# The mLSTM's two products from operands in two fp32r parts, three passes each, with one buffer a head for queries, keys and values

## The reference, cut to what matters

```
qk = silu(causal_depthwise_conv([q_m, k_m]))         # 4 taps, q and k, 1024 channels each
D[t, s]  = cumulated log gates, -inf for s > t       # per head
w[t, s]  = exp(D[t, s] - m[t]) * (q[t] . k[s]) / 16  # scores, weighted
num[t]   = sum_s w[t, s] * v[s]                      # numerators, 256 wide
den[t]   = sum_s w[t, s]
h[t]     = num[t] / max(|den[t]|, exp(-m[t]))
y_a      = sigmoid(o_pre) * layernorm_per_head(h) * g
```

## Time and profile before

| | us |
|---|---|
| median of 3 runs | 1999.2 |
| lowest and highest | 1997.16 and 2002.15 |
| the profiled execution's own time | 1996.38 |
| its span, first to last instruction | 1994.6 |
| PE busy | 1944.7 (98%) |
| DVE busy | 1050.1 (53%) |
| ACT busy | 633.4 (32%) |
| POOL busy | 280.0 (14%) |

### The profile page before, as it was taken

How to read it: one execution, slowest core, us unless ns; L and a number is a source line. 1 busy time by engine, 2 the same in 40 slices (tenths; PEclk the granted TensorE clock), 3 DMA queues, 4 the chain that set the end, 5 groups by cost and what they waited for, 6 DMA issues and landing times.

```text
span 1994.6 us, 23615 instructions
## 1 busy us (share of the span) xinstructions
PE 1944.7 (98%) x9634; PEld 1583.7 (79%) x9634; DVE 1050.1 (53%) x1458; ACT 633.4 (32%) x1054; POOL 280.0 (14%) x176
## 2 busy tenths in 40 slices
PE   7999999999999999999999999999999999999997
PEld 6778888888888888888888778777777878888885
DVE  6776543345455644343345676656676554344344
ACT  4332322233333432222234422233443333222222
POOL 2212210011111111010013000111111121011013
PEclk9999999999999999999999999999999989999998
DMA  4322233332221332323223222221111313223221
GB/s 166 98 74 85 78 92 105 95 85 77 83 64 48 121 95 95 95 95 105 94 86 100 63 74 75 96 74 55 63 59 48 116 53 106 95 96 99 93 91 66
DMA packets 53235, 172.65 MB, mean 87 GB/s; under 512 B 5995, under 2 KB 9523, under 8 KB 53128
## 3 DMA queue, kind: packets, MB, share of 16 engines
q1 hardware_dynamic: 52256, 169.93, 26.8%
q10 hardware_dynamic: 872, 1.22, 0.2%
HBM read 168.91 MB, written 2.22 MB: 86 GB/s over the span
## 4 chain that ended last, share of the span: by engine, by line
PE 87%; DVE 9%; ACT 2%; issue 1%; POOL 0%; DMA 0%; SPq 0%; DVEq 0%
PE PS L1107 26%; PE PS L1109 25%; PE PS L1108 25%; PE PS L1403 1%; PE PS L1204 1%; PE PS L1381 1%; DVE WL L1756 1%; PE PS L1425 1%; PE PS L1242 1%; PE PS L1172 1%; PE PS L1251 1%; PE PS L1265 1%; PE PS L1219 1%; DVE AR L1784 1%; DVE AR L1895 1%
## 5 line engine op out<-in xcount | busy, mean ns | idle before, releaser
L1107 PE MATMUL PS<-HH,WH 128*128 128x512 f32 x1368 | 541.0, 395 | 11.7 <-DVE WL L1756 8.3
L1109 PE MATMUL PS<-HH,WL 128*128 128x512 f32 x1368 | 534.4, 391 | 0.0
L1108 PE MATMUL PS<-HL,WH 128*128 128x512 f32 x1368 | 534.2, 390 | 0.0
L1472 ACT ACTIVATE WH<-RAW 128x1024 fp32r<-128x1024 f32 (+2 forms) x320 | 326.1, 1020 | 390.1 <-PE PS L1109 389.4
L1756 DVE TENSOR_TENSOR WL<-RAW,WH 128x1024 fp32r<-128x1024 f32 (+2 forms) x256 | 316.4, 1236 | 229.2 <-ACT WH L1472 227.4
L1107 PE MATMUL PS<-AH,WH 128*128 128x512 f32 x1096 | 433.0, 395 | 0.5 <-DVE AL L1747 0.5
L1109 PE MATMUL PS<-AH,WL 128*128 128x512 f32 x1096 | 428.1, 391 | 0.0
L1108 PE MATMUL PS<-AL,WH 128*128 128x512 f32 x1096 | 427.9, 390 | 0.0
L1107 PEld LDWEIGHTS PS<-HH,WH 128*128 128x128 f32 x1368 | 258.1, 189 | 66.9 <-DVE WL L1756 8.3
L1109 PEld LDWEIGHTS PS<-HH,WL 128*128 128x128 f32 x1368 | 257.9, 189 | 54.7
L1108 PEld LDWEIGHTS PS<-HL,WH 128*128 128x128 f32 x1368 | 258.4, 189 | 52.2
(11 more groups left out here) (238 smaller groups left out, 1417.0 us busy)
## 6 DMA issues: line engine op xcount, KB each, us to landing
RAW<-wst SPq DMA_DIRECT2D x288, 512.0 KB, 3.4
RAW<-wst SPq DMA_DIRECT2D x16, 384.0 KB, 3.0
RAW<-wst SPq DMA_DIRECT2D x16, 256.0 KB, 2.6
XT<-xT SPq DMA_DIRECT2D x3, 512.0 KB, 7.2
AR<-mx SPq DMA_DIRECT2D x4, 256.0 KB, 6.7
AR<-scr SPq DMA_DIRECT2D x16, 64.0 KB, 4.4
AR<-scr SPq DMA_DIRECT2D x8, 128.0 KB, 5.0
AR<-w SPq DMA_DIRECT2D x2, 512.0 KB, 4.2
```

Source lines behind the costliest of these rows:

```text
L1107: T.matmul(out, wh, XH[:, k, :], start=k == 0, stop=False)
L1108: T.matmul(out, wh, XL[:, k, :], start=False, stop=False)
L1109: m = T.matmul(out, wl, XH[:, k, :], start=False, stop=k == nk - 1)
L1472: t = A.activation(WH[:, i % NW, 0:n], RAW[:, i % NR, 0:n], ACT.Copy, scale=1.0)
```

## The change

Queries, keys, values and the weights of the numerators are each held as a high part (rounded to fp32r) and a low part (what is left). Each matmul of the scores and the numerators becomes three fp32r passes: high with high, high with low, low with high. The numerators have 258 columns.

- ACT rounds: `after` part 3 for qm and km (line 1569 of the changed kernel), part 1 for vm, out of PSUM (line 1575), and `weights_hi`, four instructions a head (line 1631).
- The rest is subtracted on DVE for odd km units (line 1967), for vm out of PSUM (line 1973, in place of the copy) and for `weights_lo`, four a head (line 2079), and on POOL for qm units and even km units (line 2444).
- Queries, keys and values have one buffer for all heads instead of two by turns. The roundings wait until the head before has been read.
- `weights_hi` stands one quarter after `weights`, `weights_lo` three quarters later; the numerators stay where they were.
- A flush is put ahead of each head's scores, so that part 3 is issued; one `flush_all` becomes two `flush`. Tanh gets two buffers, and waits for the low part of the unit two before.

```diff
@@ -114,7 +114,7 @@
...
-PARTS = {"qm": 2, "km": 2, "vm": 1, "om": 1, "va": 1, "ga": 1, "gb": 1, "pb": 1, "small2": 1, "gk": 1, "gv": 1,
+PARTS = {"qm": 3, "km": 3, "vm": 2, "om": 1, "va": 1, "ga": 1, "gb": 1, "pb": 1, "small2": 1, "gk": 1, "gv": 1,
@@ -128,6 +128,12 @@
 def lo_on_pool(i):
     return i in (6, 8) or i % 2 == 1 and i > 1 and UNITS[i][0] in BUSY_DVE
+
+
+def low_on_pool(i):
+
+    name, j, k0, nk = UNITS[i]
+    return name == "qm" or j % 2 == 0
 def unit_of(name, j=0, k0=0):
@@ -433,7 +439,8 @@
     e.gates_1()
     e.sum_bank("sum", 3)
     e.products(3, range(4))
-    flush_all(e)
+    flush(e)
+    flush(e)
     e.products(3, range(4, 8))
     ahead(e, 4)
     e.gates_log()
@@ -484,7 +491,11 @@
         mlstm_scores(e, h)
         fill.quarters(4)
         e.weights(h)
-        fill.quarters(12 if h else 8)
+        fill.quarters(1)
+        e.weights_hi(h)
+        fill.quarters(3)
+        e.weights_lo(h)
+        fill.quarters(8 if h else 4)
         for t in range(4):
             e.hold((*SB, OB)[t], "numer", h, t)
         e.numerators(h)
@@ -501,6 +512,7 @@
 def mlstm_scores(e, h):
     if h < 4:
+        flush(e, False)
         e.add_diagonal(h)
     if h:
         e.turn_bank("hm", h - 1, 0)
@@ -880,10 +897,17 @@
         tab, oh, vecs = part(0, 24), part(24, 1152), part(1176, 1152)
         SLOT = [part(0, 4608), part(4608, 4608)]
-        (hq0, hq1, hk0, hk1, hv0, hv1, so, xc, yc, th_, Mb, Md, vm1, WT, hm, yf_m, acol, ecol, stat, r0, r1, r2,
-         r3) = parts(4608, 1024, 1024, 1024, 1024, 1028, 1028, 1024, 516, 512, 512, 512, 512, 512, 1280, 1024, 512,
+        (_, _, _, _, _, _, so, xc, yc, th_, Mb, Md, vm1, WT, hm, yf_m, acol, ecol, stat, r0, r1, r2,
+         r3) = parts(4608, 1024, 1024, 1024, 1024, 1032, 1032, 1024, 516, 512, 512, 512, 512, 512, 1280, 1024, 512,
                      16, 16, 64, 512, 512, 512, 512)
-        hq, hk, hv = [hq0, hq1], [hk0, hk1], [hv0, hv1]
+
+        QH, QL, KH, KL = (rounded(4608 + 1024 * n, 1024) for n in range(4))
+        VH, VL = (heads_of(rounded(8704 + 1032 * n, 1032)) for n in range(2))
+        th1 = part(2328, 512)
+        wh2, wl2 = (rounded(2840 + 256 * n, 256) for n in range(2))
+        TH = [th_, th1]
+        WTH = [AH[:, 6, :], AH[:, 7, 0:384], wh2, AH[:, 7, 384:512]]
+        WTL = [AL[:, 6, :], AL[:, 7, 0:384], wl2, AL[:, 7, 384:512]]
         MX = [Mb, r3, r1, r0]
         r0, r1, r2, r3 = (x[0:4, :] for x in (r0, r1, r2, r3))
@@ -1192,21 +1222,21 @@
                 t.then_inc(*pe_done["mlstm"].next("columns_turned"))
             def scores(s, h, blocks):
-                q, k = hq[h % 2], hk[h % 2]
-                for c in (0, 1):
-                    pe.wait_ge(*at("mq", unit_of("qm", 2 * h + c)))
-                    pe.wait_ge(*at("mq", unit_of("km", 2 * h + c)))
                 for t_ in blocks:
                     x, a = SCORES[t_]
                     b, n = s.bank["scores", h, x], 512 - 128 * t_
                     s.free("scores", h, x)
                     for c in (0, 1):
-                        t = T.matmul(PS[:, b, a:a + n], k[:, c * 512 + t_ * 128:c * 512 + t_ * 128 + 128],
-                                     q[:, c * 512 + t_ * 128:c * 512 + 512], start=c == 0, stop=c == 1)
+                        keys, queries = (slice(c * 512 + t_ * 128, c * 512 + e_) for e_ in (t_ * 128 + 128, 512))
+                        pe.wait_ge(*at("m_lo", unit_of("qm", 2 * h + c)))
+                        pe.wait_ge(*at("m_hi", unit_of("km", 2 * h + c)))
+                        T.matmul(PS[:, b, a:a + n], KH[:, keys], QH[:, queries], start=c == 0, stop=False)
+                        T.matmul(PS[:, b, a:a + n], KH[:, keys], QL[:, queries], start=False, stop=False)
+                        pe.wait_ge(*at("m_lo", unit_of("km", 2 * h + c)))
+                        t = T.matmul(PS[:, b, a:a + n], KL[:, keys], QH[:, queries], start=False, stop=c == 1)
                     t.then_inc(*pe_done["mlstm"].next("scored", h, t_))
             def numerators(s, h):
-                v = heads_of(hv[h % 2])
                 pe.wait_ge(*at("ones"))
                 pe.wait_ge(*at("free", "tokens", unit_of("vm", 2 * h)))
                 pe.wait_ge(*at("free", "tokens", unit_of("vm", 2 * h + 1)))
@@ -1214,9 +1244,11 @@
                     b = s.bank["numer", h, t_]
                     s.free("numer", h, t_)
                     for x in range(t_ + 1):
-                        o = wo[x] + (t_ - x) * 128
-                        pe.wait_ge(*at("weights", h, x))
-                        t = T.matmul(PS[:, b, 0:257], WT[:, o:o + 128], v[:, x, :], start=x == 0, stop=x == t_)
+                        o = slice((t_ - x) * 128, (t_ - x) * 128 + 128)
+                        pe.wait_ge(*at("weights_lo", h, x))
+                        T.matmul(PS[:, b, 0:258], WTH[x][:, o], VH[:, x, :], start=x == 0, stop=False)
+                        T.matmul(PS[:, b, 0:258], WTH[x][:, o], VL[:, x, :], start=False, stop=False)
+                        t = T.matmul(PS[:, b, 0:258], WTL[x][:, o], VH[:, x, :], start=False, stop=x == t_)
                     t.then_inc(*pe_done["mlstm"].next("summed", h, t_))
             def gated(s, h, j):
@@ -1526,7 +1558,23 @@
                 name, j, k0, nk = UNITS[i]
                 if name in ("qm", "km") and p == 1:
                     act.wait_ge(*at("conv", i, 3))
-                    A.activation(th_, yc, ACT.Tanh, scale=0.5).then_inc(*act_done["mlstm"].next("tanh", i))
+                    if CONVS.index(i) > 1:
+                        act.wait_ge(*at("m_lo", CONVS[CONVS.index(i) - 2]))
+                    A.activation(th_of(i), yc, ACT.Tanh, scale=0.5).then_inc(*act_done["mlstm"].next("tanh", i))
+                elif name in ("qm", "km") and p == 3:
+                    h, c = j // 2, slice(j % 2 * 512, j % 2 * 512 + 512)
+                    act.wait_ge(*at("m_full", i))
+                    if h:
+                        act.wait_ge(*at("scored", h - 1, 3))
+                    t = A.activation((QH if name == "qm" else KH)[:, c], th_of(i), ACT.Copy, scale=1.0)
+                    t.then_inc(*act_done["mlstm"].next("m_hi", i))
+                elif name == "vm" and p == 1:
+                    if j > 1:
+                        act.wait_ge(*at("summed", j // 2 - 1, 3))
+                    act.wait_ge(*at("turned", i))
+                    t = A.activation(VH[:, :, j % 2 * 128:j % 2 * 128 + 128], heads_of(PS[:, s.bank["tokens", i], :]),
+                                     ACT.Copy, scale=1.0)
+                    t.then_inc(*act_done["mlstm"].next("v_hi", i))
                 elif name == "down":
                     act.wait_ge(*at("free", "sum", i))
                     s.scaled_hi("h3", AH, j, XT[:, j, :], GG[:, j:j + 1])
@@ -1565,7 +1613,7 @@
                 act.wait_ge(*at("free", "columns"))
                 act.wait_ge(*at("diagonal", h))
                 if h:
-                    act.wait_ge(*at("summed", h - 1, 3))
+                    act.wait_ge(*at("weights_lo", h - 1, 3))
                 for t_ in range(4):
                     n, o, bias = 512 - 128 * t_, wo[t_], acol[:, 4 * t_ + h:4 * t_ + h + 1]
                     t = A.activation(WT[:, o:o + 128], Md[:, 128 * t_:128 * t_ + 128], ACT.Exp, scale=-1.0, bias=bias)
...
                     t.then_inc(*act_done["mlstm"].next("exp", h, t_))
+
+            def weights_hi(s, h):
+                if h:
+                    act.wait_ge(*at("summed", h - 1, 3))
+                for t_ in range(4):
+                    n, o = 512 - 128 * t_, wo[t_]
+                    act.wait_ge(*at("weights", h, t_))
+                    t = A.activation(WTH[t_], WT[:, o:o + n], ACT.Copy, scale=1.0)
+                    t.then_inc(*act_done["mlstm"].next("weights_hi", h, t_))
             def numerators(s, h):
...
                     if p == 2:
-                        h, c = j // 2, j % 2
-                        dst = (hq if name == "qm" else hk)[h % 2][:, c * 512:(c + 1) * 512]
+                        x = th_of(i)
                         dve.wait_ge(*at("tanh", i))
-                        if h > 1:
-                            dve.wait_ge(*at("scored", h - 2, 3))
-                        t = V.scalar_tensor_tensor(out=dst, in0=th_, scalar=1.0, in1=yc, op0=ALU.add, op1=ALU.mult)
-                        t.then_inc(*dve_done["mlstm"].next("mq", i))
+                        t = V.scalar_tensor_tensor(out=x, in0=x, scalar=1.0, in1=yc, op0=ALU.add, op1=ALU.mult)
+                        t.then_inc(*dve_done["mlstm"].next("m_full", i))
+                    elif p == 3 and not low_on_pool(i):
+                        c = slice(j % 2 * 512, j % 2 * 512 + 512)
+                        dve.wait_ge(*at("m_hi", i))
+                        t = V.tensor_tensor(KL[:, c], th_of(i), f(KH[:, c]), ALU.subtract)
+                        t.then_inc(*dve_done["mlstm"].next("m_lo", i))
+                elif name == "vm":
+                    if p == 2:
```

(25 more changed lines are left out.)

13 lines of the change are left out of this document (8 added, 5 removed).

## The result

| us | before | after |
|---|---|---|
| median | 1998.4 (four executions) | 2014.5 (four executions) |
| lowest and highest | 1997.16 and 2002.15 | 2013.76 and 2015.32 |
| span of the profiled execution | 1994.6 | 2013.2 |

The changed kernel takes 16.1 us more: a ratio of 1.0079 with a 95% interval of 1.0067 to 1.0091. Forecast were 2011 and a range of 2000 to 2019, slower with a chance of 0.77.

A forecast was written before the change was run, and what follows sets the result against it. The prediction took PE, busy 98% of the span, as the bound. Its terms, -4.7 + 5.5 + 8.0 + 1.2 + 1.6 = +11.6 us, took the median from 1999.2 to 2010.8, written as 2011; range 2000 to 2019.

The forecast's parts named there:

- passes: PE's scores and numerators in all four heads: faster fp32r matmuls save 0.47 + 0.71 us a head, -4.7 us.
- end of the lead: Gate columns before head 0's scores: PE waits for bias vectors behind km1's late low part, then slow clock; +5.5 us (2.2 to 7.8).
- first numerators: Head 0's numerators: PE waits for weights_lo behind qm3's convolution on DVE, then slow clock; +8.0 us.
- later scores: Scores of heads 1 to 3: last keys need two more steps; +1.2 us in head 1, 0.8 each in heads 2 and 3.
- What bounds the kernel: Whole kernel: PE, busy 98% of the span, sets the end; DVE is about one unit late in head 0's turn.
- Numerators' passes: Numerators of each head: 30 matmuls of 258 columns at 0.121 us take 3.65 against 4.36, saving 0.71.
- rival 3: Numerators: matmuls of 258 columns cost as much as those of 512; +24 us, 2023; chance 0.07.
- Scores' passes: Scores of each head: six fp32r matmuls of each width take 3.86 us against 4.33, saving 0.47.
- The sign named for this: Scores in heads 2 and 3: line 1233 or 1236 waiting over 2 us would mean the keys' chain was underrated.
- The clock: Behind the long waits at the gate columns and head 0's numerators: granted clock about half, costing 1.4 us each.
- Rival 1: Head 0's numerators: DVE keeps up, they run at once and only the faster matmuls count; -4.7 us, 1994.5; chance 0.09.
- Rival 2: Gate columns, head 0's numerators and later scores: no new collision, waits at their lower ends; +3.7 us, about 2003; chance 0.14.

The follow-up runs named there:

- late_123: Changed kernel with all query and key low parts on DVE, head 0's weights_lo one quarter earlier, scores of heads 1 to 3 two quarters later: 2000.15 us.
- after_late: Changed kernel with only the scores of heads 1 to 3 two quarters of a unit later: 2009.02 us.
- before_late: Kernel before the change with the scores of heads 1 to 3 two quarters of a unit later: 1997.69 us.
- numer_early: Changed kernel with only the numerators in parts, scores plain fp32, and head 0's weights_lo one quarter earlier: 1998.02 us.
- lo_early: Changed kernel with head 0's weights_lo one quarter of a unit earlier, ahead of qm3's convolution on DVE: 2009.26 us.
- all_three: Changed kernel with all query and key low parts on DVE, head 0's weights_lo one quarter earlier, gate columns in their own PSUM bank: 2006.93 us.

## Why the prediction was right, and where its terms were not

The sign and the places were right, and the time lies in the range: +11.6 was forecast, +16.1 measured. The terms can be measured in the two profiled executions. PE's transposes that stand at 295.72 before, behind the last numerators, stand at 310.40 now, 14.7 later. Of that, 1.1 was there before any changed instruction, so the stage grew by 13.6: passes -4.2 (forecast -4.7), end of the lead +6.4 (5.5), first numerators +6.3 (8.0), and +5.1 is left for the later scores (2.8). Three came out above the forecast, by 0.5, 0.9 and 2.3, and one below it, by 1.7; that the sum is only 2 us off is partly luck. The other 3.9 us of the spans' difference come in code that the change does not touch. Point by point:

**What bounds the kernel.** As said: PE, with DVE about a unit late in head 0's turn.

**Numerators' passes, -0.71 a head: right.** They start 0.12 us apart in a quiet head of the kernel after:

```profile
265.42 0.28 PE L1249 MATMUL PS<-AR,AH 128*128 128x258 f32 x1
265.54 0.29 PE L1250 MATMUL PS<-AR,AH 128*128 128x258 f32 x1
265.66 0.28 PE L1251 MATMUL PS<-AR,AL 128*128 128x258 f32 x1
```

From the start of the numerators to the next transposes heads 1 to 3 got 0.77 to 0.81 us shorter. With 0.75 a head that is -3.0, and rival 3 (the price of 512 columns for 258) is out.

**Scores' passes, -0.47 a head: too much.** The blocks behind the first cost what was assumed; passes of 128 columns start 0.11 apart, nearer the floor than my 0.121:

```profile
242.61 0.28 PE L1234 MATMUL PS<-AR,AR 128*128 128x128 f32 x1
242.72 0.27 PE L1236 MATMUL PS<-AR,AR 128*128 128x128 f32 x1
242.83 0.27 PE L1233 MATMUL PS<-AR,AR 128*128 128x128 f32 x1
```

But the first block, without any wait, as in `late_123`, has passes that start 0.31 (the first), 0.24, 0.23, 0.24, 0.22 and 0.33 apart: 1.57 instead of 1.36, and the first of block 1, behind the four transposes, takes 0.26 in place of 0.17. I had put every change of operands at nothing. A head's scores take 4.04 and not 3.86, so the gain is 0.3 a head, 1.2 in all. The passes' term was -4.7; it measures -4.2 (3 x 0.75 and one for head 0 taken alike, and 4 x 0.3).

**End of the lead, +5.5: right, by partly other parts.** The rows of the kernel after, first DVE's subtraction for km1 and ACT's chain, then PE:

```profile
70.78 2.48 DVE L1967 TENSOR_TENSOR AR<-AR,AR 128x512 fp32r<-128x512 f32 x1 [0.54 <-ACT AR L1569]
...
73.90 0.63 ACT L1532 ACTIVATE AR<-AR 128x512 f32<-128x512 f32 x1 [3.15 <-DVE AR L1841]
74.43 0.46 ACT L1606 ACTIVATE AR<-PS 24x384 f32<-24x384 f32 x1
```

```profile
74.95 0.26 PE L1220 MATMUL PS<-C,AR 4*128 4x4 f32 x1 [4.35 <-ACT AR L1606]
```

The chain is the one described: the subtraction waits for ACT's rounding, meets POOL's split (0.69 becomes 2.48), and eviction, tanh and vector 1 follow. PE waited 4.35 for vector 1 (5.1 forecast) and not at all for vector 0 (1.3 forecast); a collision costs 0.9 and not 1.3. Then the clock stood at half: 3.4 us of loss where I had 1.4, part of it during the wait. Scores of head 0 start 6.3 us later than before, 5.2 of that without the 1.1 us by which the two executions differed from the start. The first of these scores still run at the lower clock; at the transposes behind them it is 6.1, and 6.4 without the shorter passes. So a wait that was priced too long and a clock that was priced too short made up for each other.

**First numerators, +8.0: the place was right, the wait 2.8 too long.** PE's wait is 4.79, against 7.6:

```profile
96.28 0.68 DVE L1841 TENSOR_TENSOR AR<-PS,RB 128x512 f32<-128x512 f32 x1
97.00 2.41 DVE L1948 TENSOR_SCALAR AR<-AR,COL 128x512 f32<-128x512 f32 x1
99.44 3.21 DVE L1952 SCALAR_TENSOR_TENSOR AR<-AR,COL 128x512 f32<-128x512 f32 x3
102.56 1.16 DVE L2079 TENSOR_TENSOR AL<-AR,AH 128x512 fp32r<-128x512 f32 x2
```

```profile
103.39 0.55 PE L1249 MATMUL PS<-AR,AH 128*128 128x258 f32 x1 [4.79 <-DVE AL L2079]
```

The length of DVE's chain was priced well: from the eviction at 96.28 to PE's start 7.1 us, forecast 4.3 + 0.6 + 2.0 = 6.9. What failed is "PE's own delay and DVE's are the same there". PE would have been at the numerators at 98.60, 7.3 later than before; DVE started the eviction only 5.0 later than at 91.27. So 2.3 us of the chain was over when PE came. I had added 2.8 us of DVE's delay from the values to PE's. But when DVE evicted qm2 at 87.77, the values done, PE had only just finished its sum (24 passes of 0.227 from 82.03 end at 87.5): PE had come late itself, and the 2.8 us were part of its delay once more. From the transposes behind head 0's scores to those behind its numerators PE lost 5.6 us against before (7.2 to 12.8), 6.3 without the shorter passes: the term measures +6.3, within its 5.7 to 9.0.

**Later scores, +1.2 and +1.6: too small.** PE waited three times, and gave up the cover that I had counted:

```profile
129.10 0.50 PE L1233 MATMUL PS<-AR,AR 128*128 128x512 f32 x1 [2.60 <-ACT AR L1569]
...
184.98 0.50 PE L1233 MATMUL PS<-AR,AR 128*128 128x512 f32 x1 [1.01 <-ACT AR L1569]
...
239.26 0.50 PE L1233 MATMUL PS<-AR,AR 128*128 128x512 f32 x1 [1.00 <-ACT AR L1569]
```

PE did not get to do five passes first, as I wrote. It did three, since the second half of the width is asked for by its high part already, and these three are under 1 us of cover. In heads 2 and 3 the wait is the 0.8 that I took, plus 0.2 and the restart of the passes. In head 1 it is 2.6 against 1.8 before, and the clock falls behind it, which it had not done before. `after_late` and `late_123` put the term at 4.3 to 5.8 us, net of what the kernel before gains by the same edit; the forecast had 2.8. The sign named for this, a wait of over 2 us in heads 2 and 3, did not show; the term was too small all the same.

**The clock is the term that was mis-sized most.** The forecast named falls only behind the two long waits, at 1.4 each. Measured in the two profiled executions are four more falls of 1.7 in this stage, 6.8 against 2.8, and two in code that the change does not touch, 3.4. The waits grew by 12.0, where the forecast has 13.5 in its terms without their clock (4.1, 6.6 and 2.8). So it is the clock by which the stage came out longer than forecast. The other 3.4 cannot be put down to the change: `before_late`, whose edit ends with the stage as well, lost 10.2 us in that code, against 8.6 in the kernel before.

**Rivals.** Rival 1 (DVE keeps up) fell; `numer_early` shows, for the numerators alone, what it would have taken, a place one quarter earlier, and that the gain is then eaten by small waits and a fall. With scores in parts no kernel came below the kernel before. Rival 2 (small waits, 2003) fell at the columns, 4.3 against its 2.2.

**What stays open.** The falls in untouched code took 8.5 to 12.0 us in these profiles. Executions of one kernel differ in clock too: those of the kernel before ran from 1996.14 us at a mean granted clock of 0.992 to 2002.64 at 0.989. In the profiled executions the same code with the same wait of 2.95 us at 40 to 44 was followed by one fall in the changed kernel and by two in `lo_early`. What decides whether a fall comes, no run tells. So the ledger's clock entry holds for one execution and is uncertain by a few microseconds for a median, as `all_three` shows. No version in two parts beats the kernel before; the best with both products is `late_123` (1.0004), and `numer_early`, which has the numerators alone, equals the kernel before. `before_late`, which only moves scores, is at 0.9989 [0.998, 0.9997], a gain at the edge of what can be measured.

## What to carry to other kernels

Where PE is the bound and is 97% busy, replacing slow passes with faster ones that need extra elementwise steps trades a saving on PE for steps on chains that PE waits for; price the chain at each place where the consumer stands close behind its last producer, and move the consumer there first. Price a new wait on PE with the clock behind it: here each fall was worth 1.7 us, as much as a small wait. Split the change by product: one half cost 3.1 us and became neutral by one edit of place, the other cost 10.8.
